# Gates of the second block by one Strassen step, inside its attention

## What is computed

```python
proj = h @ w_in
(dq, dk, dv, sq, sk, sv, mq, mk, mv, g_diff, g_sb, g_moba) = split(proj)
a_out = rms_norm(diff_attention(dq, dk, dv, lam, cos, sin), diff_g) * (1 - lambda_init)
b_out = stick_breaking_attention(sq, sk, sv)
c_out = moba_attention(mq, mk, mv, cos, sin)
merged = (sigmoid(g_diff) * (a_out @ w_diff_o) + sigmoid(g_sb) * (b_out @ w_sb_o)
          + sigmoid(g_moba) * (c_out @ w_moba_o))
return merged @ w_out
```

## Time and profile before

| what | value |
|---|---|
| median of three runs | 3542.71 us |
| the profiled execution, its own time | 3545.56 us |
| its span, first to last instruction | 3543.7 us |
| PE busy, of the span | 3392.9 us, 96% |
| PE weight loads busy | 2972.6 us, 84% |
| DVE busy | 2051.4 us, 58% |
| ACT busy | 662.0 us, 19% |
| POOL busy | 182.8 us, 5% |
| granted TensorE clock, mean | 0.980 |
| chain that ended last, by engine | PE 90%, DVE 6%, ACT 2%, DMA 1% |

### The profile page before, as it was taken

One profiled execution on the slowest core, in us unless ns is written; L12 is line 12 of the kernel. 1 busy time (PEld: TensorE's weight loads), 2 busy tenths in 40 slices (PEclk: granted clock), 3 DMA queues, 4 the chain that ended last, 5 costly groups with the idle time before them and its releaser, 6 DMA issues.

```text
span 3543.7 us, 51820 instructions
## 1 busy us (share of the span) xinstructions
PE 3392.9 (96%) x21526; PEld 2972.6 (84%) x21526; DVE 2051.4 (58%) x4159; ACT 662.0 (19%) x1561; POOL 182.8 (5%) x140
## 2 busy tenths in 40 slices
PE   7999999998999989989999999999999999999998
PEld 4887655787888878868999999987899899987898
DVE  2478463455554166664798675534575775434574
ACT  2111342012221011142121111023111111033111
POOL 0000000003543300000000000000000000000000
PEclk8999999999999999999999999999999999999999
DMA  5244102222223334503444444432344444432453
GB/s 215 78 164 169 36 12 72 84 84 72 89 90 116 134 110 177 195 14 118 167 165 162 154 169 140 165 120 95 131 168 166 143 167 144 149 125 97 137 171 120
DMA packets 65465, 450.19 MB, mean 127 GB/s; under 512 B 7120, under 2 KB 10192, under 8 KB 13648
## 3 DMA queue, kind: packets, MB, share of 16 engines
q1 hardware_dynamic: 65232, 446.88, 36.4%
HBM read 445.80 MB, written 1.05 MB: 126 GB/s over the span
## 4 chain that ended last, share of the span: by engine, by line
PE 90%; DVE 6%; ACT 2%; DMA 1%; issue 1%; SPq 0%; DVEq 0%; ACTq 0%
PE bank L1171 61%; PE bank L907 14%; PE bank L1340 3%; PE bank L1422 2%; PE bank L955 2%; PE bank L1025 1%; DVE conv_sum L2404 1%; PE bank L973 1%; PE bank L1050 1%; PE bank L1464 1%; DMA residual<-in_x 1%; PE bank L1126 1%; PE bank L1104 1%; DMA weight_ring<-w_q 1%; DVE normed L2067 0%
## 5 line engine op out<-in xcount | busy, mean ns | idle before, releaser
L1171 PE MATMUL bank<-normed,weight_ring 128*128 128x128 f32 (+1 forms) x5472 | 766.3, 297 | 22.7 <-ACT normed L1597 12.1
L1171 PEld LDWEIGHTS bank<-normed,weight_ring 128*128 128x128 f32 x5472 | 710.5, 193 | 72.3 <-issue 39.0
L1171 PE MATMUL bank<-normed,mixer_small 128*128 128x128 f32 (+1 forms) x3040 | 385.2, 281 | 3.6 <-DVE normed L2773 3.6
L1171 PEld LDWEIGHTS bank<-normed,mixer_small 128*128 128x128 f32 x3040 | 364.5, 192 | 9.4 <-issue 4.6
L907 PE MATMUL bank<-normed,weight_ring 128*128 128x256 f32 (+1 forms) x1088 | 295.3, 421 | 0.4 <-ACT region_a L1683 0.3
L1171 PE MATMUL bank<-region_a,weight_ring 128*128 128x128 f32 (+1 forms) x2128 | 294.6, 293 | 0.7 <-DVE region_a L2359 0.6
L1171 PEld LDWEIGHTS bank<-region_a,weight_ring 128*128 128x128 f32 x2128 | 272.1, 192 | 16.6 <-issue 7.1
L907 PEld LDWEIGHTS bank<-normed,weight_ring 128*128 128x128 f32 x1088 | 200.3, 190 | 75.5 <-issue 54.4
L1171 PE MATMUL bank<-turned,weight_ring 128*128 128x256 f32 (+1 forms) x944 | 199.0, 354 | 0.0
L1171 PEld LDWEIGHTS bank<-turned,weight_ring 128*128 128x128 f32 x944 | 163.7, 191 | 18.2
L1171 PE MATMUL bank<-region_a,mixer_small 128*128 128x128 f32 (+1 forms) x1232 | 160.5, 283 | 0.0
(11 more groups left out here) (308 smaller groups left out, 4702.0 us busy)
## 6 DMA issues: line engine op xcount, KB each, us to landing
weight_ring<-w_ada SPq DMA_DIRECT2D x48, 1024.0 KB, 6.5
weight_ring<-w_up SPq DMA_DIRECT2D x44, 1024.0 KB, 4.9
weight_ring<-w_f1up SPq DMA_DIRECT2D x44, 1024.0 KB, 4.8
weight_ring<-w_f2up SPq DMA_DIRECT2D x44, 1024.0 KB, 4.8
weight_ring<-w_gt SPq DMA_DIRECT2D x32, 1024.0 KB, 4.8
weight_ring<-w_qk SPq DMA_DIRECT2D x24, 1024.0 KB, 4.9
weight_ring<-w_v SPq DMA_DIRECT2D x20, 1024.0 KB, 4.9
weight_ring<-w_pj SPq DMA_DIRECT2D x16, 1024.0 KB, 4.8
```

The source lines that it names most:

```text
L1171: mm = nc.tensor.matmul(bank[u.bank][:, pair.columns(p)], lhs(k), rhs(k), start=begins and p in pair.opens and k == 0, stop=ends and p in ...
```

## The change

The gates become twelve pairs (two gates each) by `seven`, the weight block of a pair as its 2 x 2 quarters, the activation differences those that the qk stage left in `hn`. The seven products of a pair are spread over the same four places in two steps: in the even step 1, 2 ahead of the turn and 7, 6 behind it, in the odd step 5 ahead and 3, 4 behind. The y bank is bank 6, the x bank is bank 7. ScalarE copies product 1 alone, once a pair, to two new places (`gate_one`). VectorE gets the four sums of each pair and its two combinations. Two pairs' sums and the first combination of pair 0 stand ahead of its loop; at the end of each even step n it makes the last combination of pair (n + 4) / 2 - 1 and then the sums of pair (n + 4) / 2 + 1, and at the end of each odd step the first combination of that step's pair. The last sums are in step 16, the last combination in step 20. The counting of the sums ring changes with it (24 in place of 12 per layer).

The diff, cut to its core:

```diff
 plan.gate2(g):
         if g % 2 == 0:
             self.take_blocks("gt2", "gt2", 1, SLOT, g // 2)
-        self.take_at("gt2", 6 + g % 2)
-        self.blocks["gt2"][-1].after = self.units["gt2"][-1]
+            for z in range(2):
+                self.take_at("gt2", 6 + z)
+            self.blocks["gt2"][-1].after = self.units["gt2"][-1]
+            self.pairs.setdefault("gt2", []).append(Pair(self.units["gt2"][-2:], P, False))
...
+        gate_one = cut(turned_t, 0, 2, P)
...
 TensorE:
-            def seven(b, s, pair, n, act, made, used, begins, ends, l=0, ring=wsum, midway=None):
+            def seven(b, s, pair, n, act, made, used, begins, ends, l=0, ring=wsum, midway=None, part=slice(0, 7)):
...
-                waited = 0
-                landed(b, 0, l)
-                for x, p in enumerate(pair.order):
+                waited = max([sums_before.get(p, 0) for p in pair.order[:part.start]] + [0])
+                if part.start == 0:
+                    landed(b, 0, l)
+                for x, p in enumerate(pair.order[part]):
...
+                gate_act = Halves(hn, lambda k: hn[:, k, 0:P], lambda k: hn[:, 4 + k, 0:P], lambda k: hn[:, k, P:2 * P],
+                                  0, KD // 2, X0, P, lambda what, k: None, lambda k: hn[:, 4 + k, P:2 * P])
                 def gate_half(g, half):
-                    ...
+                    at_ = [0, 2, 4, 5, 7]
+                    x = 2 * (g % 2) + half
+                    seven(plan.blocks["gt2"][g // 2], (base + 12 + g // 2) % SUM_RING, plan.pairs["gt2"][g // 2], KD // 2,
+                          gate_act, sums_made, sums_used, True, True, l, part=slice(at_[x], at_[x + 1]))
...
 ScalarE:
-                def first_product(j, y, before):
+                def first_product(j, y, before, place=one2):
...
                 def gate_copy(g):
-                    u = plan.units["gt2"][g]
-                    full_bank(u, 0, l)
-                    a_(gates2[g // KD][:, g % KD, :], bank[u.bank][:, 0:SEQ], ACT.Copy).then_inc(bank_free[u.bank], 1)
+                    if g % 2 == 0:
+                        first_product(g // 2, plan.units["gt2"][g], plan.units["gt2"][g - 4] if g >= 4 else None, gate_one)
...
 VectorE:
+                    paired2 += [(b, KD // 2) for b in plan.blocks["gt2"]]
-            FFN2 = FK + 3 * KD // 2 + 12
+            GATES2 = FK + 3 * KD // 2 + 12
+            FFN2 = GATES2 + 12
...
+                def gate_first(p):
+                    mix_y(p, plan.units["gt2"][2 * p], gates_of(p), gate_one)
+
+                def gate_last(p):
+                    mix_x(plan.units["gt2"][2 * p], plan.units["gt2"][2 * p + 1], gates_of(p))
+
+                sums(GATES2)
+                sums(GATES2 + 1)
+                gate_first(0)
                 for n in range(-2, 24):
...
+                    p = (n + 4) // 2
+                    if p <= 12 and n % 2 == 0:
+                        gate_last(p - 1)
+                        if p + 1 < 12:
+                            sums(GATES2 + p + 1)
+                    elif p < 12:
+                        gate_first(p)
```

More of the change, by code:

```diff
@@ L1376, in ffn @@
                 norm_sums(f"f{f}pre", X0, l)
[L1377 removed]
+                base = (DEPTH + 2 * l + f - 1) * (FK + 3 * KD // 2) + 24 * (l + f - 1)
                 for j, b in enumerate(plan.blocks[f"f{f}up"]):
@@ L1408, in layer2 @@
                 norm_sums("mpre", X0, l)
-                base = (DEPTH + 2 * l + 1) * (FK + 3 * KD // 2) + (l + 1) * 12 - 12
+                base = (DEPTH + 2 * l + 1) * (FK + 3 * KD // 2) + l * 24
                 for j, b in enumerate(plan.blocks["qk2"]):
@@ L1920, in first_product @@
                         emptied(act, before, l)
-                    a_(one2[:, j % 2, :], bank[y.bank][:, 0:P], ACT.Copy).then_inc(one_copied, 1)
+                    a_(place[:, j % 2, :], bank[y.bank][:, 0:P], ACT.Copy).then_inc(one_copied, 1)
                 def up(name):
@@ L2783, in halves, with mix_y @@
                         V.sent(turned_ready)
-                def mix_y(j, y, dst):
+                def mix_y(j, y, dst, place=one2):
                     dve.wait_ge(one_copied, V.next(one_copied))
@@ L2790, in mix_y @@
                     v.tensor_tensor(seg[:, 0:2], bank[y.bank][:, P:3 * P].rearrange("p (s c) -> p s c", c=P),
-                                    one2[:, j % 2, :].unsqueeze(1).to_broadcast([P, 2, P]), ALU.add).then_inc(mix_step, 1)
+                                    place[:, j % 2, :].unsqueeze(1).to_broadcast([P, 2, P]), ALU.add).then_inc(mix_step, 1)
                     dve.wait_ge(mix_step, V.at(mix_step, V.sent(mix_step)))
@@ L2981, in store, with gates_of @@
                     v.tensor_copy(ob2[:, tile_, :], bank[u.bank][:, 0:SEQ]).then_inc(bank_free[u.bank], 1)
+                def gates_of(p):
+                    return gates2[2 * p // KD][:, 2 * p % KD:2 * p % KD + 2, :].rearrange("p a c -> p (a c)")
+                def gate_first(p):
[5 more added lines that the diff above has]
+                gate_first(0)
                 for n in range(-2, 24):
```

## The result

The changed kernel takes 3570.4 us (median of 4 runs, 3566.7 to 3571.36) against 3543.74 us before: a ratio of 1.0077, with a 95% interval of 1.0062 to 1.0092. That is 26.7 us slower. I had forecast 8.8 us slower, with a range that ended at 3562. The sign was right, the size was not.

The account below looks back on a forecast made before the run. TensorE was taken to set the pace to step 20, then the round trip over VectorE and ScalarE. Terms -2.64 + 2.27 + 0.4 + 3.6 + 0.8 gave +4.4 us a layer, +8.8 for two: 3551.5 us, range 3541 to 3562.

Parts of the forecast that it names:

- What TensorE saves: Gate products: a pair takes 6.25 us in place of 7.00, about 0.7 us saved a pair, 17 us at most.
- What VectorE gets: Added to VectorE per pair: four sums (2.52 us) and two combinations (0.66 and 0.80), together 3.98 us.
- The estimate of +3.4 a layer by the table: Alternative price of VectorE's four sums, 2.38 us at 594 ns each: +3.4 us a layer instead of +4.4.
- The walk: Longest chain through the attention stage between TensorE's score products: +4.4 us a layer, stage from 128.1 to about 132.4 us.
- Scores 10: Score product 10 in the stage, counted from the start of the gates: no more than 0.7 us earlier than before.
- Scores 18 to 20: Late in the stage, where the last sums are queued behind product 17's exponent: these score products lie 13 us apart.
- the clock: Rival, chance 0.12: TensorE's lower clock behind new gaps at turns 8, 12, 14, 18 costs up to 13 us, 3564 us.

Follow-up runs that it names:

- e1: The changed kernel with 1 to 7 idle-time matmuls filling TensorE's longest waits for VectorE: 3543.24 us, ratio 1.0001.
- e3: The changed kernel with VectorE's sums for the next pair moved from the even steps to the end of the odd steps: 3547.68 us, ratio 1.0012.
- e7: The changed kernel with the gates' four sums made by GpSimd in place of VectorE, nothing filled: 3550.79 us, ratio 1.0018.
- e2: The kernel before the change with idle-time matmuls ahead of turns 22 and 23 and of values: 3536.91 us, ratio 0.9984.
- e5: The changed kernel with sums at the end of the odd steps and idle-time matmuls at turns 12, 14, 22, 23 and last values: 3529.03 us, ratio 0.9964.

## Why the prediction was right in its chain and wrong in its size

- **What TensorE saves** was right: 6.3 us for a pair ahead of the loop instead of 7.0, and 0.89 for each product at full clock.
- **What VectorE gets** was right: the sums take 2.62 us (2367.53 to 2369.46 + 0.69), 2.61 in the earlier trace rows. The instruction in its new place costs what it cost in the old one, and the 594 ns that I worked out from the Trainium skill's table ("VectorE: DVE Perf Modes", section on the TRN2 errata) are too low for the 0.69 measured. Below the table the same section corrects itself: for an fp32 addition of two tensors it gives (N + 151) / 0.96, which is 691 ns for 512 columns, and the row agrees. I had read the table and not that line. The estimate of +3.4 a layer by the table was too high besides: it set 4 x 594 ns, durations in full, against 2.52, which has the overlap taken off. Like with like is 2.38 against 2.74, and the estimate would be about +1.5.
- **The walk** was right. Its stage of 132.4 us carries the slow stretch that the tail had before. With the clock held by filling, the stage is 131.2 against 126.5: 4.6 us a layer, forecast 4.4. Scores 10 was "no more than 0.7 earlier": 0.2 earlier with the gaps filled. Scores 18 to 20 were to lie 13 us apart: 13.4 filled, 15.1 not.
- **The step that failed** is the clock, which I priced at zero in the sum and kept as a rival with 0.12. It was worth 15.3 us in the two stages. The rival's price was right: up to 1.6 us for each new gap, at turns 8, 12, 14 and 18, 13 us in all and 3564. The runs show 1.5 to 1.7 us at each of those eight places (the changed kernel against e1, from one scores product to the next), 13.2 us in all, and 1.2 and 0.5 us more in the two tails, where the gap ahead of turn 22 grew from 2.60 to 3.4 us. The chance was wrong, and the prediction gives no reason for it. The kernel before had the evidence in the earlier trace rows, a slow stretch behind its gap of 2.60 us. It had more that the prediction does not name: a slow stretch behind the 1.82 us shown above, and gaps of 1.25 and 1.31 us at turns 12 and 14 with none (eight records of 256 columns behind them take 1.89 us, as at full clock). The Trainium skill ("TensorE: Matmul & The Clock Gate", section on HAM oscillation) says that waits for DMA between bursts of matmuls put the array back to half clock over and over; the waits of its case are longer than those here. Behind the shorter waits for VectorE it holds for all ten gaps of 2.08 us and more in the two stages of the profile after, and not for 7 of the 20 gaps of 2.08 to 2.19 us counted above.
- **What stays open.** The filling gained 8 us more in the whole than in the two stages, and 2 to 3 us more in the kernel before. The lower clock that goes on behind the stage explains some of it. How the rest is spread over the program, where runs of one kernel differ by several us, was not tried. Why one gap of 2.1 us brings the lower clock and another does not is open too.

## What to carry to other kernels

When a change moves work from TensorE to an engine that TensorE waits for, walk the chain from one handover to the next; and where the walk opens new gaps of about 2 us in TensorE's order (here 1.82 us was enough once, and 1.44 brought nothing), price each with the slow stretch that rows of the same kernel show behind such a gap, in the sum and not beside it. Put preparatory work, which is needed a whole step later, behind the result for which the other engine waits next and not ahead of it: that move alone was worth 23 us here. To tell waiting from clock, fill the gaps with matmuls without use; it is a cheap experiment, and here it is a gain of 0.2% even for the unchanged kernel.

## What the runs showed of the hardware

- A gap of 2.1 us in TensorE's work can go by at full clock or bring a slow stretch in the same execution (e3: 2.09 us in both layers, 0.96 and 0.95 mean clock, stages of 127.0 and 129.3 us). Over five kernels 13 of 20 gaps of 2.08 to 2.19 us brought one. A gap of 1.82 us brought one in the kernel before; gaps of 1.44 us (e7) brought none.
- Matmuls without use in the gaps held the granted clock at 1.00 through the stage (e1, e2, e5).
- Beside a sum of GpSimd on SBUF tiles, VectorE's TENSOR_SCALAR over 256 columns of an SBUF tile took 1.37 us in place of 0.35 (e7); with GpSimd idle it kept its 0.35. Additions of a PSUM bank stayed at 0.42 and reductions of an SBUF tile at 0.41 beside a sum.
